# Differential attention: the first softmax map left undivided, the row norm's epsilon scaled to match, and the second map's separate scaling folded into the difference

## The chip, the cores and the metric

The kernel runs as one program on one core of a Trainium2 chip. Its time is the device time of one execution in microseconds (us). Three runs of the kernel before took 1530.87, 1522.81 and 1524.97 us; their median is 1524.97 us.

## The reference, cut to what matters

The network layer has three attention branches; the change is in branch A, differential attention, with 4 heads and 2 softmax maps each, over two groups of 512 tokens.

```python
logits = jnp.einsum('bqhmd,bkhmd->bhmqk', qb, k) * scale + bias
p = jax.nn.softmax(logits, axis=-1)
attn = p[:, :, 0] - lam * p[:, :, 1]
o = jnp.einsum('bhqk,bkhe->bqhe', attn, v)
o = rms_norm(o, subln_g) * (1.0 - lambda_init)   # mean square over 128 values, plus EPS = 1e-6
```

`lam` is one number for the layer. The softmax of a map is `exp(logits - max)` divided by the row's sum `z`; call the exponentials `e0`, `e1` and their sums `z0`, `z1`. Each row of `attn` is `e0/z0 - lam * e1/z1`. The row norm that follows divides by the root of the row's mean square, so a factor on a whole row falls out of it if EPS is multiplied by the square of that factor.

## The kernel before, in words

The work is written out by hand for five engines, each with its own list of instructions in `build_program`; they meet at semaphores. TensorE (PE) multiplies, ScalarE (ACT) takes exponentials and rounds operands to their high parts, VectorE (DVE) takes maxima, normalises and forms low parts, GpSimd (POOL) forms the low parts of weights (L450) and inverse roots (L436), SyncE (SP) issues the loads and stores. Every product is three products of high and low parts.

Branch A is a loop over 4 units (one head each, both its maps). Units 0 to 2 are a hardware loop, in which the counts that semaphores are compared with, and addresses that depend on the unit, come from registers; unit 3 is written out behind it. A unit goes through 8 tiles `t` of 128 query rows (4 in each token group), with two slots (`t % 2`) for scores and row statistics (`stat`). For one tile:

- PE: `score` (L611) makes the scores of both maps in PSUM.
- DVE: `find_max` adds the bias and takes each map's maximum (two instructions of L1383, into `s`), and L1388 negates the two maxima.
- ACT: `exp_probs` (L1017) takes both exponentials and, by an accumulator, the sums `z0`, `z1` (`stat` columns 4 and 5).
- DVE: `scales` takes both reciprocals (L1394, columns 6 and 7), waits for them (`steps.done`), and multiplies the second by `lam` (L1397, column 8).
- ACT: `scale_second` (L1038) multiplies the second map by column 8.
- DVE: `norm_probs` (L1411) waits for that (`scaled`) and writes `e0 * column 6 - scaled second map` in place of `e0`.
- PE: `turn_tile` turns the result into PSUM in four transposes (L618); ACT rounds it (`probs_hi`, L1029) and DVE takes the rest (`probs_lo`, L1355).
- PE: `mix` (L633) multiplies with the values, one token group at a time.

The order on the engines around it, in `attend_qkv`:

- DVE, step `t`: `scales(t-1)`, `find_max(t)`, `norm_probs(t-1)`, `probs_lo(t-2)`. At `t = 1` the low parts of the values follow (`v_lo`, L1355).
- ACT, step `t`: `probs_hi(t-2)`, `scale_second(t-1)`, `exp_probs(t)`; behind `exp_probs(3)` a weight block is rounded (`split_w`, L1002), and POOL's L450 follows from it.
- PE, step `t`: `turn_tile(t-2)`, `score(t+1)`, then shares of the gate's projection (L581), as many blocks as `GATE_SHARES_A = [1, 1, 2, 1, 1, 1, 1, 0]` says. After step 7 `finish` sets the next unit's projections between the last two `turn_tile`s.

`find_max(t)` may write its slot of `s` once tile `t-2` has been turned (`p_turned`). After each unit, PE sums the squares of the outputs (L720) and DVE copies 8 columns of sums to `a_ss` (L1486, an address that depends on the unit in the loop). After unit 3 `mean_square` (L1366) makes `a_ss / 128 + EPS` in one instruction on 32 columns, POOL raises it to the power -0.5 (L436), and DVE spreads the result over diagonals (L1634) that PE multiplies (L819).

Branches B and C (`both` is true) have two separate softmax maps. They use the same helpers, with `scale_second` (L1038) and a `norm_probs` of their own (L1408).

Of the kernel before, what the change touches and what calls it, by code (L numbers as in the profile page):

```python
# [28 lines left out]
ALU = mybir.AluOpType  # L29
# [3 lines left out]
P = 128  # L33
# [11 lines left out]
UNITS = 4  # L45
# [6 lines left out]
EPS = 1e-6  # L52
LAMBDA_INIT = 0.2
SCALE = HD ** -0.5
NEG = -3.0e38
LEAD = 8
# [22 lines left out]
def build_program(nc, w_qkvg_a, w_qg_b, w_qkvg_c, w_gates, w_branch, w_out, w_pg, w_pe,  # L79
# [3 lines left out]
    with ExitStack() as ctx:  # L83
# [25 lines left out]
        ident = sb("ident", [P, P])  # L109
        mask = sb("mask", [P, 3, 48])  # L110
        stat = sb("stat", [P, 2, 12])
        small = sb("small", [P, 128])
        ps = ctx.enter_context(nc.psum_tensor("ps", [P, 8, 512], F32))

        bias = tables[:, 0:2 * NBIAS].rearrange("p (e n) -> p e n", e=2)
# [3 lines left out]
        lambda_in = tables[:, 256:256 + 4 * HD]  # L119
        copy_of_x = [tables[:, c * TOK:(c + 1) * TOK] for c in range(2)]  # L120
        neg_half = small[:, 0:1]
        lam = small[:, 1:2]
        subg = small[:, 2:3]
        ones2 = small[:, 4:6]
        lam_sum = small[:, 6:8]
# [3 lines left out]
        a_ss = small[:, 32:64]  # L129
        a_rstd = small[:, 64:96]  # L130
        head_ss, head_rstd = small[:, 96:112], small[:, 112:128]

        const_in = sem("const_in")
        x_in = [sem(f"x_in{i}") for i in range(4)]
# [436 lines left out]
        def _(pe):  # L571
# [77 lines left out]
            def turn_tile(u, t, near, both):  # L649

                pe.wait_ge(normed, LEAD + 8 * u + t + 1)
                if both:

                    pe.wait_ge(pt0_ready, half_count(u, t, 0, both))
                    turn_probs(t, near, both, 0).then_inc(p0_turned, 1)
                    pe.wait_ge(scaled, LEAD + 8 * u + t + 1)
                    pe.wait_ge(pt_ready, half_count(u, t, 1, both))
                    turn_probs(t, near, both, 1).then_inc(p_turned, 1)
                else:
                    pe.wait_ge(pt_ready, LEAD + 8 * u + t - 1)  # L660
                    turn_probs(t, near, both, 0).then_inc(p_turned, 1)
# [326 lines left out]
        def _(act):  # L988
# [40 lines left out]
                    nc.scalar.copy(*turned_probs(pt_hi, j, near, both, e)) \  # L1029
                        .then_inc(pt0_hi_done if half0 else pt_hi_done, 1)  # L1030

            def scale_second(u, t, near, both):

                lo, hi = C_KEYS[t % QT] if near else (0, QT)
                act.wait_ge(scales_ready, LEAD + 8 * u + t + 1)
                p1 = s[:, t % 2, 1, 0:(hi - lo) * P]
                factor = stat[:, t % 2, 7:8] if both else stat[:, t % 2, 8:9]
                nc.scalar.mul(p1, p1, factor).then_inc(scaled, 1)  # L1038

            def gate_tanh(u, n_gate, bank):  # L1040
                act.wait_ge(block_done, LEAD + n_gate + 1)
# [26 lines left out]
            def attend_qkv(u, n, uses, near, both, gate_at, n_turned):  # L1068

                act.wait_ge(y_ready, LEAD + 2 * u)  # L1070
                save_plain(n + 2, 0, vg[:, :])
                for t in range(8):
                    if t >= 2:
                        probs_hi(u, t - 2, near, both)
                    if t >= 1:
                        scale_second(u, t - 1, near, both)
                    exp_probs(u, t, near, both)
                    if t == 0:
                        values_hi(u, n_turned, 0, both)
                    if t == 3:  # L1080
                        split_w(n + 4, 0, uses + 1)
                    if t == gate_at:
                        gate_tanh(u, n + 3, 2)
                    if t == gate_at + 1:
                        split_w(n + 5, 1, uses + 1)

            def finish(u, n, uses, near, both, gate_at):
                if gate_at == 8:
                    gate_tanh(u, n + 3, 2)
                    split_w(n + 5, 1, uses + 1)  # L1090
                scale_second(u, 7, near, both)
                probs_hi(u, 6, near, both)
                probs_hi(u, 7, near, both)

# [119 lines left out]
            def attend_b(i, last):  # L1214
                u = UNITS + i
                n, uses = N_B + 2 * i, N_B // 2 + 2 + i
                for t in range(8):
                    if t >= 2:
                        probs_hi(u, t - 2, False, True)
                    if t >= 1:  # L1220
                        scale_second(u, t - 1, False, True)
                    if t == 3 and not last:
                        act.wait_ge(rope_turned, LEAD + 2 + i)
                        save_plain(n, 2, rope_buf)
                    if t == 4 and not last:
                        square_heads(UNITS + 4 + i, 2, y_row(i + 1))
                    exp_probs(u, t, False, True)
                    if t == 1:
                        split_w(n + 1, 0, uses)
                    if t == 5 and not last:  # L1230
                        split_w(n + 2, 1, uses)
                scale_second(u, 7, False, True)
                probs_hi(u, 6, False, True)
                probs_hi(u, 7, False, True)
                gate_tanh(u, n + (0 if last else 1), 4)
                if last:
                    split_w(n + 2, 1, uses)
                if not last:
                    act.wait_ge(rope_turned, LEAD + 3 + i)
                    q_to_hi(u + 1, 6)  # L1240
# [112 lines left out]
        def _(dve):  # L1353
# [36 lines left out]
            def scales(u, t, both):  # L1390

                st = stat[:, t % 2, :]
                dve.wait_ge(exped, LEAD + 8 * u + t + 1)
                done = nc.vector.reciprocal(st[:, 6:8], st[:, 4:6])  # L1394
                if not both:
                    steps.done(dve, done)
                    done = nc.vector.tensor_tensor(st[:, 8:9], st[:, 7:8], lam, ALU.mult)  # L1397
                done.then_inc(scales_ready, 1)

            def norm_probs(u, t, near, both):  # L1400

                lo, hi = C_KEYS[t % QT] if near else (0, QT)
                width = (hi - lo) * P
                st = stat[:, t % 2, :]
                p0, p1 = s[:, t % 2, 0, 0:width], s[:, t % 2, 1, 0:width]
                if both:
                    dve.wait_ge(scales_ready, LEAD + 8 * u + t + 1)
                    nc.vector.tensor_scalar(p0, p0, st[:, 6:7], None, ALU.mult).then_inc(normed, 1)  # L1408
                else:
                    dve.wait_ge(scaled, LEAD + 8 * u + t + 1)  # L1410
                    stt(out=p0, in0=p0, scalar=st[:, 6:7], in1=p1, op0=ALU.mult, op1=ALU.subtract) \  # L1411
                        .then_inc(normed, 1)

            def probs_lo(u, j, near, both):
# [120 lines left out]
            nc.vector.tensor_reduce(lam_sum, prod, AX.X, ALU.add).then_inc(lam_summed, 1)  # L1535
            steps.done(dve, nc.vector.tensor_scalar(subg, subg, 1.0 - LAMBDA_INIT, None, ALU.mult))
            dve.wait_ge(lam_exped, LEAD + 1)
            steps.done(dve, nc.vector.tensor_tensor(lam, lam_exp[:, 0:1], lam_exp[:, 1:2], ALU.subtract))
            steps.done(dve, nc.vector.tensor_scalar(lam, lam, LAMBDA_INIT, None, ALU.add))

            def h_lo_part(t):
                dve.wait_ge(h_hi_done, LEAD + t + 1)
# [22 lines left out]

            first_qkv(0, 0)
            with dve.Fori(0, UNITS - 1) as i:
                steps.loop(i, 8 + 8)
                dve.wait_ge(bias_ready, LEAD + i + 1)
                attend_qkv(i, False, False, 8, i)  # L1570
                finish(i, False, False, 8)
                next_qkv(i, i, i, True)
                save_squares(i)
# [6 lines left out]
                take_y(last, last, g, True)  # L1580
            save_squares(last)
            dve.wait_ge(ss_saved, LEAD + UNITS)
            mean_square(a_ss, P, a_var)

            def rope_tables(n_in):
                dve.wait_ge(rope_in, 16 * n_in)
# [311 lines left out]
```

## Time and profile before

| what | value |
|---|---|
| median of the three runs | 1524.97 us |
| lowest and highest run | 1522.81 and 1530.87 us |
| span of the profiled execution | 1522.4 us |
| PE busy | 1411.3 us, 93% of the span, 6780 instructions |
| DVE busy | 602.4 us, 40%, 1062 instructions |
| ACT busy | 536.9 us, 35%, 977 instructions |
| POOL busy | 291.8 us, 19%, 173 instructions |
| mean granted TensorE clock | 0.973 of full speed |

The span runs from the first to the last instruction of one profiled execution; for that execution the page gives no other time. It lies 0.41 us below the lowest run and 2.57 us below the median. A busy share is an average over the whole program; what an edit in one stage is worth is read from that stage's own stretch.

In the answers of the trace, "idle before <-X" is how long the engine stood still ahead of an instruction and whose end released it. In the chain of waits, "issue" is time in which the engine waited for nothing that the profile shows.

### The profile page before, as it was taken

The page shows a single profiled execution, that of the slowest core. Times are in us where ns is not written, and L with a number is a line of the kernel's source. Part 1 is how long each engine was busy: PE and PEld are TensorE (multiplying, and loading weights), DVE is VectorE, ACT ScalarE, POOL GpSimd, SP SyncE. Part 2 cuts the span into 40 slices and gives each one's busy share as a digit, 9 for nine tenths or more (in the row PEclk, how much of TensorE's full clock was granted, in tenths as well). Part 3 has the DMA queues.
Part 4 walks back from the last instruction along what each step waited for, and adds up shares of the span by engine and source line. Part 5 has one row for each costly group of instructions (what it writes and reads, how often), then busy time and mean ns, then how long its engine had stood idle before and what let it go on. Part 6 is the DMA issues. An engine that isn't in the chain of part 4 may idle for free.

```text
span 1522.4 us, 18598 instructions
## 1 busy us (share of the span) xinstructions
PE 1411.3 (93%) x6780; PEld 1129.2 (74%) x6780; DVE 602.4 (40%) x1062; ACT 536.9 (35%) x977; POOL 291.8 (19%) x173
## 2 busy tenths in 40 slices
PE   5999999999999798987999898989898999899998
PEld 3767677677887576765788786878787888788887
DVE  5272635546300646456212125152525212544332
ACT  4262534432111536446211115252524212324432
POOL 1211202131222113020022131111211112213100
PEclk9999999999999999998999999999999999999999
DMA  5111101011111000000011110111000113322200
GB/s 185 57 36 36 49 21 49 28 45 46 42 42 55 28 14 28 14 14 8 21 43 61 55 56 23 46 34 34 34 28 29 42 42 138 111 82 70 69 35 35
DMA packets 25746, 71.77 MB, mean 47 GB/s; under 512 B 2872, under 2 KB 4792, under 8 KB 25568
## 3 DMA queue, kind: packets, MB, share of 16 engines
q1 hardware_dynamic: 25696, 71.09, 13.9%
q8 instruction: 33, 0.54, 0.2%
q14 instruction: 17, 0.14, 0.0%
HBM read 66.86 MB, written 4.23 MB: 47 GB/s over the span
## 4 chain that ended last, share of the span: by engine, by line
PE 84%; DVE 8%; ACT 3%; issue 3%; POOL 1%; DMA 0%; SPq 0%; DVEq 0%; ACTq 0%; POOLq 0%
PE ps L581 45%; PE ps L738 9%; PE ps L633 7%; PE ps L952 6%; PE ps L934 6%; PE ps L618 3%; PE ps L611 3%; ACT s L1017 2%; DVE s L1383 2%; PE ps L598 2%; PE ps L958 1%; DVE pt_lo L1355 1%; DVE stat L1388 1%; PE ps L764 1%; POOL small L436 1%
## 5 line engine op out<-in xcount | busy, mean ns | idle before, releaser
L450 POOL TENSOR_TENSOR w_lo<-stage,w_hi 128x1024 fp32r<-128x1024 f32 (+1 forms) x92 | 194.4, 2113 | 923.8 <-ACT w_hi L1002 922.6
L581 PE MATMUL ps<-h_hi,w_hi 128*128 128x512 f32 x1040 | 335.8, 404 | 4.2 <-ACT s L1017 1.9
L581 PE MATMUL ps<-h_lo,w_hi 128*128 128x512 f32 x1040 | 324.3, 393 | 0.0
L581 PE MATMUL ps<-h_hi,w_lo 128*128 128x512 f32 x1040 | 323.7, 393 | 0.0
L581 PEld LDWEIGHTS ps<-h_hi,w_hi 128*128 128x128 f32 x1040 | 188.6, 189 | 59.2 <-issue 19.7
L581 PEld LDWEIGHTS ps<-h_lo,w_hi 128*128 128x128 f32 x1040 | 196.5, 189 | 44.5
L581 PEld LDWEIGHTS ps<-h_hi,w_lo 128*128 128x128 f32 x1040 | 196.3, 189 | 43.3
L1002 ACT CAST w_hi<-stage 128x1024 fp32r<-128x1024 f32 (+1 forms) x92 | 86.0, 935 | 298.2 <-PE ps L581 213.1
L1029 ACT CAST pt_hi<-ps 128x512 fp32r<-128x512 f32 (+2 forms) x160 | 77.6, 525 | 167.6 <-PE ps L618 103.6
L1355 DVE TENSOR_TENSOR pt_lo<-ps,pt_hi 128x512 fp32r<-128x512 f32 (+2 forms) x160 | 91.3, 603 | 113.9 <-ACT pt_hi L1029 113.9
L618 PE MATMUL ps<-ident,s 128*128 128x128 f32 x544 | 85.6, 288 | 51.5 <-DVE pt_lo L1355 34.4
L618 PEld LDWEIGHTS ps<-ident,s 128*128 128x128 f32 x544 | 63.9, 146 | 80.7 <-DVE pt_lo L1355 32.1
L1383 DVE CUSTOM_DVE_ANT_0 s<-ps,tables 128x512 f32<-128x512 f32 (+2 forms) x128 | 70.5, 588 | 91.3 <-PE ps L611 64.0
L1017 ACT ACTIVATE s<-s,stat 128x512 f32<-128x512 f32 (+2 forms) x128 | 81.2, 636 | 55.0 <-DVE stat L1388 54.6
L1502 DVE SCALAR_TENSOR_TENSOR s<-s,ps 128x1024 f32<-128x1024 f32 x16 | 19.5, 1221 | 190.1 <-PE ps L738 190.1
L633 PE MATMUL ps<-pt_hi,v_hi 128*128 128x512 f32 (+2 forms) x192 | 71.0, 370 | 9.1 <-DVE pt_lo L1355 4.8
L738 PE MATMUL ps<-pt_hi,w_hi 128*128 128x512 f32 x192 | 61.7, 404 | 10.3 <-DVE m L1504 8.9
L633 PE MATMUL ps<-pt_lo,v_hi 128*128 128x512 f32 (+2 forms) x192 | 69.1, 360 | 0.0
L633 PE MATMUL ps<-pt_hi,v_lo 128*128 128x512 f32 (+2 forms) x192 | 68.6, 357 | 0.0
L1038 ACT ACTIVATE s<-s,stat 128x512 f32<-128x512 f32 (+2 forms) x96 | 65.0, 677 | 4.4 <-DVE stat L1394 4.4
L738 PE MATMUL ps<-pt_hi,w_lo 128*128 128x512 f32 x192 | 60.9, 399 | 0.0
L738 PE MATMUL ps<-pt_lo,w_hi 128*128 128x512 f32 x192 | 60.7, 398 | 0.0
(173 smaller groups left out, 1881.6 us busy)
## 6 DMA issues: line engine op xcount, KB each, us to landing
stage<-in_w_gates SPq DMA_DIRECT2D x24, 512.0 KB, 3.2
stage<-in_w_qkvg_a SPq DMA_DIRECT2D x19, 512.0 KB, 3.2
stage<-in_w_qkvg_c SPq DMA_DIRECT2D x16, 512.0 KB, 3.2
stage<-in_w_branch SPq DMA_DIRECT2D x24, 256.0 KB, 2.7
m<-in_x_tok SPq DMA_DIRECT2D x4, 1024.0 KB, 9.4
y<-in_x_tok SPq DMA_DIRECT2D x8, 512.0 KB, 3.4
stage<-in_w_pg SPq DMA_DIRECT2D x16, 256.0 KB, 2.7
out<-y SPq DMA_DIRECT2D x16, 256.0 KB, 2.0
```

Of the source, the lines that this page charges most:

```text
L450: nc.gpsimd.tensor_tensor(dst, stage[:, slot, 0:width], f32(hi), ALU.subtract).then_inc(w_ready, 1)
L581: done = mm(ps[:, bank + g, :], w[:, slot, k * P:(k + 1) * P], h[:, k, g * SEQ:(g + 1) * SEQ], start=first and part == 0, stop=last and pa ...
L618: done = nc.tensor.transpose(ps[:, e if both else t % 2, k * P:(k + 1) * P], s[:, t % 2, e, k * P:(k + 1) * P], ident[:, :])
L633: done = mm(ps[:, 2 + g, q0 * P:q1 * P], v[:, g * QT + k, e * HD:e * HD + P], p[:, e if both else g, k, q0 * P:q1 * P], start=n == 0, stop ...
L738: done = mm(ps[:, 2 + g, :], w[:, slot, c * P:(c + 1) * P], yy[:, c * TOK + g * SEQ:c * TOK + (g + 1) * SEQ], start=c == 0 and part == 0, ...
L934: done = mm(ps[:, 2 * c + nb, :], a[:, k * P:(k + 1) * P], w[:, k, nb * 512:(nb + 1) * 512], start=k == 0 and part == 0, stop=k == KC - 1 ...
L952: mm(ps[:, c, :], a[:, k * P:(k + 1) * P], w[:, k * 512:(k + 1) * 512], start=k == 0 and part == 0, stop=k == KC - 1 and part == 2)
L1002: nc.scalar.copy(dst, stage[:, slot, 0:width]).then_inc(w_hi_done, 1)
L1017: done = nc.scalar.activation(dst, src, ACT.Exp, bias=stat[:, t % 2, 2 + e:3 + e], accum_out=stat[:, t % 2, 4 + e:5 + e])
L1029: nc.scalar.copy(*turned_probs(pt_hi, j, near, both, e)) \
L1355: sub = lambda out, whole, hi: nc.vector.tensor_tensor(out, whole, f32(hi), ALU.subtract)
L1383: done = nc.vector.tensor_tensor_reduce(out=s[:, t % 2, e, 0:width], in0=ps[:, 4 + 2 * (t % 2) + e, 0:width], in1=bias[:, e, first:first + ...
```

## The change

For branch A (`both` false):

- `scales` takes the reciprocal of `z1` alone, then `z0 * (-lam) * (1/z1)` into column 8, then `z0 * z0` into a new column of `a_z`, at an address that depends on the unit and the tile. It waits for the first two results, one after the other; `scales_ready` is signalled by the third.
- `scale_second` is no longer issued on ACT for this branch.
- `norm_probs` writes `e1 * column 8 + e0` in place of `e0`, without the wait for `scaled`.
- Behind the branch, `mean_square` on `a_ss` becomes two instructions with a wait between them: `a_z * EPS`, then `a_ss / 128 + a_z`.
- `lam` is kept negated; `small` grows from 128 to 160 columns; the counts of `scaled` begin at branch B; the loop's step count per unit goes from 16 to 24.

For branches B and C the instructions are the same.

```diff
-        small = sb("small", [P, 128])
+        small = sb("small", [P, 160])
...
+        a_z = small[:, 128:160]
...
-                    pe.wait_ge(scaled, LEAD + 8 * u + t + 1)
+                    pe.wait_ge(scaled, LEAD + 8 * (u - UNITS) + t + 1)
...
-                factor = stat[:, t % 2, 7:8] if both else stat[:, t % 2, 8:9]
-                nc.scalar.mul(p1, p1, factor).then_inc(scaled, 1)
+                nc.scalar.mul(p1, p1, stat[:, t % 2, 7:8]).then_inc(scaled, 1)
...
-                    if t >= 1:
-                        scale_second(u, t - 1, near, both)
+                    if t >= 1 and both:
+                        scale_second(u, t - 1, near)
...
-                done = nc.vector.reciprocal(st[:, 6:8], st[:, 4:6])
-                if not both:
-                    steps.done(dve, done)
-                    done = nc.vector.tensor_tensor(st[:, 8:9], st[:, 7:8], lam, ALU.mult)
-                done.then_inc(scales_ready, 1)
+                if both:
+                    nc.vector.reciprocal(st[:, 6:8], st[:, 4:6]).then_inc(scales_ready, 1)
+                    return
+
+                steps.done(dve, nc.vector.reciprocal(st[:, 7:8], st[:, 5:6]))
+                steps.done(dve, stt(out=st[:, 8:9], in0=st[:, 4:5], scalar=neg_lam, in1=st[:, 7:8], op0=ALU.mult,
+                                    op1=ALU.mult))
+                nc.vector.tensor_tensor(a_z[:, bass.ds(8 * u + t, 1)], st[:, 4:5], st[:, 4:5], ALU.mult) \
+                    .then_inc(scales_ready, 1)
...
-                    dve.wait_ge(scaled, LEAD + 8 * u + t + 1)
-                    stt(out=p0, in0=p0, scalar=st[:, 6:7], in1=p1, op0=ALU.mult, op1=ALU.subtract) \
+                    stt(out=p0, in0=p1, scalar=st[:, 8:9], in1=p0, op0=ALU.mult, op1=ALU.add) \
...
-                steps.loop(i, 8 + 8)
+                steps.loop(i, 8 + 16)
...
-            mean_square(a_ss, P, a_var)
+            steps.done(dve, nc.vector.tensor_scalar(a_z, a_z, EPS, None, ALU.mult))
+            stt(out=a_ss, in0=a_ss, scalar=1.0 / P, in1=a_z, op0=ALU.mult, op1=ALU.add).then_inc(a_var, 1)
```

## Rows read from the trace of the kernel before

**Rows 1.** Engines by stretch: branch A's four units; busy us (instructions), then PEclk, DMA, GB/s.
```profile
core 0: us, PE busy (x) PEld busy (x) DVE busy (x) ACT busy (x) POOL busy (x), PEclk, DMA share, GB/s
68.61:139.97 71.36, 67.81 (x323) 52.44 (x322) 33.77 (x78) 32.24 (x60) 11.88 (x6) 0.95 0.11 38
139.97:209.38 69.41, 64.92 (x323) 50.12 (x322) 33.95 (x79) 31.18 (x59) 11.88 (x6) 1.00 0.11 38
209.38:280.63 71.25, 67.66 (x323) 52.16 (x322) 33.95 (x79) 31.24 (x59) 11.88 (x6) 0.95 0.10 33
280.63:334.95 54.32, 50.34 (x261) 38.25 (x261) 32.02 (x80) 28.19 (x56) 8.18 (x6) 1.00 0.13 42
```

**Rows 2.** Waits of PE, 68 to 340 us: us in total, times, longest us.
```profile
PE ps L618 <- DVE s L1411: 9.0, 8, 1.8
PE ps L618 <- DVE v_lo L1355: 6.6, 4, 1.7
```

**Rows 3.** Timeline of unit 1, tiles 4 to 6: start us, us, engine, line, operation.
```profile
163.46 0.72 ACT L1017 ACTIVATE s<-s,stat 128x512 f32<-128x512 f32 x1 [0.91 <-DVE stat L1388]
...
165.01 0.17 DVE L1394 RECIPROCAL stat<-stat 128x2 f32<-128x2 f32 x1 [0.33 <-ACT s L1017]
165.22 0.16 DVE L1397 TENSOR_TENSOR stat<-stat,small 128x1 f32<-128x1 f32 x1
165.41 0.72 ACT L1038 ACTIVATE s<-s,stat 128x512 f32<-128x512 f32 x1
165.49 0.69 DVE L1383 CUSTOM_DVE_ANT_0 s<-ps,tables 128x512 f32<-128x512 f32 x1
...
166.92 0.74 DVE L1411 SCALAR_TENSOR_TENSOR s<-s,stat 128x512 f32<-128x512 f32 x1
...
167.72 0.66 PE L618 MATMUL ps<-ident,s 128*128 128x128 f32 x4 [0.45 <-DVE s L1411]
```

**Rows 4.** Instructions of L1411: who it waited for, us in total and times.
```profile
  ACT s L1038: 1.4, 4
```

**Rows 5.** Instructions of L1486: those of its sequencer; ns min/median/max.
```profile
L1486 DVEq FUSED_REGOPS  x3: 57/57/57, 140.0 to 280.7; - x3
```

**Rows 6.** Timeline, where `find_max` waits for PE: unit 1 (tiles 2, 3), units 0, 2 (6).
```profile
149.07 0.69 DVE L1383 CUSTOM_DVE_ANT_0 s<-ps,tables 128x512 f32<-128x512 f32 x1 [0.70 <-PE ps L618]
...
153.35 0.69 DVE L1383 CUSTOM_DVE_ANT_0 s<-ps,tables 128x512 f32<-128x512 f32 x1 [0.81 <-PE ps L618]
...
96.09 0.69 DVE L1383 CUSTOM_DVE_ANT_0 s<-ps,tables 128x512 f32<-128x512 f32 x1 [0.46 <-PE ps L618]
...
236.75 0.69 DVE L1383 CUSTOM_DVE_ANT_0 s<-ps,tables 128x512 f32<-128x512 f32 x1 [0.43 <-PE ps L618]
```

**Rows 7.** Timeline of unit 0, tiles 3 and 4, beside POOL's weight split.
```profile
86.72 0.17 DVE L1394 RECIPROCAL stat<-stat 128x2 f32<-128x2 f32 x1 [0.34 <-ACT s L1017]
...
87.70 2.37 POOL L450 TENSOR_TENSOR w_lo<-stage,w_hi 128x1024 fp32r<-128x1024 f32 x1 [25.60 <-ACT w_hi L1002]
...
87.82 0.69 DVE L1383 CUSTOM_DVE_ANT_0 s<-ps,tables 128x512 f32<-128x512 f32 x1
...
88.55 1.55 DVE L1388 TENSOR_SCALAR stat<-stat 128x2 f32<-128x2 f32 x1
```

**Rows 8.** Chain that ended last: unit 3's start, and behind branch A: start us, us.
```profile
286.73 0.65 DVE s L1411
287.38 1.15 DVE v_lo L1355
...
334.69 0.19 DVE small L1366
...
334.95 5.43 POOL small L436
```

**Rows 9.** Timeline of unit 3, tile 7, beside POOL's weight split (begun at 314.15).
```profile
314.73 2.38 DVE L1411 SCALAR_TENSOR_TENSOR s<-s,stat 128x512 f32<-128x512 f32 x1 [0.34 <-ACT s L1038]
```

**Rows 10.** Chain that ended last, unit 0: the same six L581 matmuls at either clock.
```profile
92.48 2.86 PE ps L581 x6
...
96.81 1.59 PE ps L581 x6
```

More of the change, by code:

```diff
@@ L121, in build_program @@
         neg_half = small[:, 0:1]
-        lam = small[:, 1:2]
+        neg_lam = small[:, 1:2]
         subg = small[:, 2:3]
@@ L1030, in probs_hi, with scale_second @@
                         .then_inc(pt0_hi_done if half0 else pt_hi_done, 1)
-            def scale_second(u, t, near, both):
+            def scale_second(u, t, near):
                 lo, hi = C_KEYS[t % QT] if near else (0, QT)
@@ L1090, in finish @@
                     split_w(n + 5, 1, uses + 1)
-                scale_second(u, 7, near, both)
+                if both:
+                    scale_second(u, 7, near)
                 probs_hi(u, 6, near, both)
@@ L1220, in attend_b @@
                     if t >= 1:
-                        scale_second(u, t - 1, False, True)
+                        scale_second(u, t - 1, False)
                     if t == 3 and not last:
@@ L1231, in attend_b @@
                         split_w(n + 2, 1, uses)
-                scale_second(u, 7, False, True)
+                scale_second(u, 7, False)
                 probs_hi(u, 6, False, True)
@@ L1393, in scales @@
                 dve.wait_ge(exped, LEAD + 8 * u + t + 1)
-                done = nc.vector.reciprocal(st[:, 6:8], st[:, 4:6])
-                if not both:
-                    steps.done(dve, done)
-                    done = nc.vector.tensor_tensor(st[:, 8:9], st[:, 7:8], lam, ALU.mult)
-                done.then_inc(scales_ready, 1)
+                if both:
+                    nc.vector.reciprocal(st[:, 6:8], st[:, 4:6]).then_inc(scales_ready, 1)
[5 more added lines that the diff above has]
+                    .then_inc(scales_ready, 1)
             def norm_probs(u, t, near, both):
@@ L1537, in _ @@
             dve.wait_ge(lam_exped, LEAD + 1)
-            steps.done(dve, nc.vector.tensor_tensor(lam, lam_exp[:, 0:1], lam_exp[:, 1:2], ALU.subtract))
-            steps.done(dve, nc.vector.tensor_scalar(lam, lam, LAMBDA_INIT, None, ALU.add))
+            steps.done(dve, nc.vector.tensor_tensor(neg_lam, lam_exp[:, 1:2], lam_exp[:, 0:1], ALU.subtract))
+            steps.done(dve, nc.vector.tensor_scalar(neg_lam, neg_lam, -LAMBDA_INIT, None, ALU.add))
             def h_lo_part(t):
```

## The prediction, made before the changed kernel was run

> **What bounds the kernel now.** I read the page's engine shares first (PE is busy nearly throughout), then cut out the stretch that the change touches. The table of engines by stretch gives branch A's four units 266.3 us together, of which PE is busy 250.7 us [rows 1]. So 15.6 us of PE idleness is all that the change could ever win back there, apart from the clock: units 0 and 2 show a mean granted clock of 0.95 and last 71.36 and 71.25 us, unit 1 shows 1.00 and lasts 69.41 us.
>
> Next, who makes PE wait. It is always the transpose L618: 9.0 us in 8 waits for the difference L1411 and 6.6 us in 4 waits for the values' low part, which stands behind L1411 on DVE [rows 2]. Which engine makes L1411 late? The timeline of one tile shows a ring [rows 3]: the exponentials start at 163.46, both are over when the reciprocal starts at 165.01, L1397 follows at 165.22, `find_max` of the next tile at 165.49, then its negation, then the next tile's exponentials and L1411 at 166.92, and PE, idle for 0.45 us, turns at 167.72. What the reader should see is where L1038 lies: ACT runs it from 165.41 to 166.13, while DVE is inside `find_max`, and L1411 can't start before `find_max` is over anyway. ACT itself stands idle 0.91 us ahead of the exponentials, waiting for DVE. So the ring is DVE's small operations, `find_max` and the two exponentials; the scaling is beside it.
>
> **The change, part by part.**
>
> *L1038 removed, 32 times 0.72 us of ACT* [rows 3]. Worth nothing: its cover is `find_max`, and with the multiplication gone ACT waits longer for L1388. L1411 waited for it 1.4 us in 4 waits [rows 4], one per unit, at tile 7; there PE has two half projections to do before it needs the result, and L1411 is held by POOL's split in any case (2.38 us instead of 0.74, with POOL's instruction under way) [rows 9]. Bounds: 0 to 1.4 us gained; I take 0. The wait for `scaled` that goes with it was already met when L1411 came up. `norm_probs` stays one instruction of the same form and size: no change.
>
> *`scales` becomes longer, between the exponentials and `find_max`: this is in the ring.* Reciprocal, wait, L1397 was two dependent small operations; now there are three, two of them awaited. From the start of the reciprocal to the start of L1397 is 165.22 - 165.01 = 0.21 us, wait included [rows 3]. The new product with `-lam` costs that step once more: 0.21 us. The square has an address that depends on the unit: the one such instruction of this engine nearby has a register operation of 0.057 us ahead of it, in the 3 units of the loop only [rows 5]. The trace has no small instruction of this form, with a register operation between a wait and its start; lower end 0 (the register work hidden under the instruction before), upper end 0.11 us (it and as much again to start). I take 0.10. So a tile costs 0.31 us more in units 0 to 2 and 0.21 in unit 3.
>
> Not every tile pays. Which of `scales(0)` to `scales(5)` reach PE?
> - `scales(0)`: `find_max(1)`, L1411, the values' low part and PE's first turn follow without a gap (the end of that run is in the chain) [rows 8]. Paid in all 4 units.
> - `scales(1)` and `scales(2)`: `find_max` behind them stands idle 0.70 and 0.81 us for PE's transpose [rows 6]. The usual gap there is 165.49 - 165.38 = 0.11 [rows 3], so 0.59 and 0.70 us are free, more than 0.31. Hidden; if PE came sooner they would be paid.
> - `scales(3)`: the reciprocal starts at 86.72, POOL's weight split at 87.70, and L1388 then takes 1.55 us in place of 0.17 [rows 7]; all four units look so. L1388 ends when POOL does, and POOL's start hangs on the exponentials of tile 3, ahead of this `scales`. So 0.31 us goes into a hold of 1.38 us. Hidden.
> - `scales(4)` and `scales(5)`: in units 1 and 3 the ring is tight (rows 3 are such a tile): both paid. In units 0 and 2 PE runs half as fast here (six matmuls take 2.86 us, later 1.59 [rows 10]), and `find_max(6)` waits 0.46 and 0.43 us for it [rows 6], so 0.35 and 0.32 of the 0.62 us is free and 0.27 and 0.30 is paid.
> - `scales(6)` and `scales(7)`: PE has the unit's last projections to do. Hidden.
>
> Sum: units 0 and 2: 0.31 + 0.27 and 0.31 + 0.30; unit 1: 3 x 0.31 = 0.93; unit 3: 3 x 0.21 = 0.63. Together 2.8 us. With the register work at 0 it is 0.28 + 0.30 + 0.63 + 0.63 = 1.8 us, at 0.11 it is 2.9.
>
> *Behind branch A*, one instruction of 0.19 us ahead of the inverse roots becomes two with a wait, in the chain that ends last [rows 8]: 0.2 us more. The powers are of larger numbers now; the trace shows no dependence on the values, so their 5.43 us stays.
>
> *Semaphore counts, `neg_lam`, the larger tile*: set-up or bookkeeping of the same number of instructions elsewhere; 0.
>
> Total +3.0 us. On the profiled execution that is 1522.4 + 3.0 = 1525.4 us of span; this execution stands 2.57 us under the median of the runs, so the median should be 1524.97 + 3.0 = **1528.0 us**, 0.2% more. About 0.5% (7.6 us) is what a measurement of this kernel can tell from no change, so the forecast is no change.
>
> **The rivals.**
>
> *1. The clock falls in other units.* Units 0 and 2 lose 71.3 - 69.4 = 1.9 us to a clock that falls to 1.2 GHz after PE's idle time behind the first turns; unit 1, with nearly the same gaps, loses none [rows 1]. The new small waits lengthen gaps and shift them. If units 1 and 3 fall too, they pay 3.8 us but hide about half of their 1.6: some 1531.0 us. If units 0 and 2 stop falling, 3.8 us comes back and they pay 0.93 each in place of 0.6: 1524.9. For: the units alternate although their work is equal. Against: nothing in the change aims at it.
>
> *2. A new small operation is caught by POOL's weight split: slower.* Place: `scales(3)`. The square must have started before POOL does, 87.70 - 86.72 = 0.98 us after the reciprocal [rows 7]; I put it 0.52 us after. If it comes later than 0.98 us, it is held until POOL ends at 90.07, and `find_max(4)` with 1.35 us behind it, instead of L1388 alone; L1388 would end near 91.8 in place of 90.10, 1.7 us late in each of four units: 3.0 + 6.8 = 9.8 us, 1534.8. For: L1411, two inputs in SBUF, was held so [rows 9]. Against: 0.46 us of room, and `find_max` beside POOL is not held (0.69 us) [rows 7].
> The Trainium skill, "SBUF — State Buffer", section "Who interferes with whom", says that a VectorE instruction with two SBUF inputs contends with a GpSimd instruction that reads SBUF, and that the one that issues second fully blocks. Both new products are of that kind, and the row of the held L1411 agrees with it; by this rule they are safe only because they come first.
>
> *3. ACT was in the ring after all: faster.* If the scaling set L1411 at the tight tiles (3 in each unit), 12 x 0.72 = 8.6 us would come back, less the 3.0: 1519.4. Against: ACT's 0.91 us of idleness and DVE's order of work [rows 3].
>
> *4. Nothing hides: slower.* If the room behind PE and POOL is not there, 24 tiles pay 0.31 and 8 pay 0.21: 9.1 us, 1534.3. Against: rows 6 and 7.
>
> **How the numbers follow.** Forecast 0.66; clock falls added 0.10, falls lost 0.09; rival 2 0.05; rival 3 0.04; rival 4 0.04; 0.02 for what I don't see. Forecast and both clock cases end within 0.5% of 1524.97 (1517.3 to 1532.6). Rivals 2 and 4 end just beyond it: slower 0.09; faster 0.05; same 0.86. The range takes the forecast's bounds (1526.8 to 1528.1, less the 1.4 us at tile 7), both clock cases (1524.9 to 1531.0) and, since three runs of one program lay 8 us apart, some 2.5 us on either side: 1522.5 to 1533.5.
>
> **What would show it.** In the changed profile: three small DVE instructions between the exponentials and `find_max`, from the reciprocal's start to `find_max` some 0.8 us in the loop, where it was 0.48 (165.49 - 165.01); the second and third start 0.2 and 0.5 us after the first. ACT idle some 1.6 us ahead of the exponentials in place of 0.91. L1411's successor at tile 5 later against the unit's start by 0.6 to 0.9 us. Units of 71.9, 70.3, 71.9 and 54.9 us if the clock keeps its pattern. L1388 of tile 4 still ends with POOL. It is wrong if a unit becomes shorter at the same clock, if `find_max(4)` starts behind POOL, or if branches B and C change by more than the clock explains.

## The result, and the profile after

Six runs of the changed kernel took 1529.95 to 1535.46 us, median 1532.46; six of the kernel before on the same chip took 1522.81 to 1530.87, median 1524.95. The ratio is 1.0043, with a 95% interval from 1.0024 to 1.0061: slower by 0.2% to 0.6%. The prediction was 1528.0 us, with a range that ends at 1533.5.

The two profiled executions differ by 1528.2 - 1522.4 = 5.8 us of span. The table of engines by stretch shows branch A's four units of the changed kernel, to be held against [rows 1], with the same columns:

```profile
68.19:140.32 72.13, 67.81 (x323) 52.08 (x322) 35.40 (x86) 27.35 (x52) 11.87 (x6) 0.95 0.12 38
140.32:212.38 72.06, 66.45 (x323) 51.09 (x322) 35.64 (x87) 26.10 (x51) 11.86 (x6) 0.98 0.11 37
212.38:283.84 71.46, 67.85 (x323) 52.29 (x322) 35.63 (x87) 26.45 (x51) 11.87 (x6) 0.95 0.10 33
283.84:339.12 55.28, 51.76 (x263) 39.51 (x263) 34.03 (x89) 23.28 (x48) 8.16 (x5) 0.97 0.13 41
...
338.00:360.00 22.00, 19.76 (x110) 17.09 (x110) 13.55 (x40) 2.07 (x2) 10.62 (x3) 0.92 0.00 1
```

The units grew by 0.77, 2.65, 0.21 and 0.96 us, 4.6 together. Two things are mixed in that. PE's idle time in them went from 15.6 to 270.9 - 253.9 = 17.1 us, 1.5 more; PE's busy time for the same matmuls went from 250.7 to 253.9 us, 3.1 more, nearly all of it in units 1 and 3, whose granted clock is now 0.98 and 0.97 where it was 1.00. The last row is mostly the stretch behind branch A (the spread of the inverse roots, from 339.12 on), with a clock of 0.92. That stretch took 1.3 us longer than before. The start of the program gave 0.4 back; branches B and C differ by 0.3.

PE's waits in branch A (us in total, times, longest), against 9.0 in 8 and 6.6 in 4 before [rows 2]:

```profile
PE ps L619 <- DVE s L1415: 9.7, 8, 1.9
PE ps L619 <- DVE v_lo L1356: 7.3, 4, 2.1
```

The timeline (start us, us, engine, line, operation, idle time before) at three places: POOL's hold in unit 0, the ring in unit 1, the same tile in unit 3.

```profile
77.76 0.69 DVE L1384 CUSTOM_DVE_ANT_0 s<-ps,tables 128x512 f32<-128x512 f32 x1 [0.38 <-PE ps L619]
...
86.62 0.17 DVE L1399 RECIPROCAL stat<-stat 128x1 f32<-128x1 f32 x1 [0.34 <-ACT s L1018]
...
87.18 0.16 DVE L1402 TENSOR_TENSOR small<-stat 128x1 f32 x1
87.48 0.69 DVE L1384 CUSTOM_DVE_ANT_0 s<-ps,tables 128x512 f32<-128x512 f32 x1
87.60 2.37 POOL L451 TENSOR_TENSOR w_lo<-stage,w_hi 128x1024 fp32r<-128x1024 f32 x1 [25.93 <-ACT w_hi L1003]
...
88.82 1.18 DVE L1389 TENSOR_SCALAR stat<-stat 128x2 f32<-128x2 f32 x1
...
163.68 0.17 DVE L1399 RECIPROCAL stat<-stat 128x1 f32<-128x1 f32 x1 [0.33 <-ACT s L1018]
163.88 0.22 DVE L1400 SCALAR_TENSOR_TENSOR stat<-stat,small 128x1 f32<-128x1 f32 x1
164.24 0.16 DVE L1402 TENSOR_TENSOR small<-stat 128x1 f32 x1
164.53 0.69 DVE L1384 CUSTOM_DVE_ANT_0 s<-ps,tables 128x512 f32<-128x512 f32 x1
...
165.88 0.17 DVE L1389 TENSOR_SCALAR stat<-stat 128x2 f32<-128x2 f32 x1
165.96 0.75 DVE L1415 SCALAR_TENSOR_TENSOR s<-s,stat 128x512 f32<-128x512 f32 x1
166.09 0.72 ACT L1018 ACTIVATE s<-s,stat 128x512 f32<-128x512 f32 x1 [1.97 <-DVE stat L1389]
...
167.64 0.17 DVE L1399 RECIPROCAL stat<-stat 128x1 f32<-128x1 f32 x1 [0.33 <-ACT s L1018]
...
305.21 0.17 DVE L1399 RECIPROCAL stat<-stat 128x1 f32<-128x1 f32 x1 [0.33 <-ACT s L1018]
...
305.86 0.69 DVE L1384 CUSTOM_DVE_ANT_0 s<-ps,tables 128x512 f32<-128x512 f32 x1
```

In the ring [rows 3] the reciprocal now starts 164.53 - 163.68 = 0.85 us ahead of `find_max` (L1384), where it was 0.48, and ACT stands idle 1.97 us ahead of the exponentials, where it was 0.91 (the prediction said some 1.6). One ring, from reciprocal to reciprocal, lasts 167.64 - 163.68 = 3.96 us. In unit 3, which has no address from a register, the reciprocal starts 305.86 - 305.21 = 0.65 us ahead of `find_max`. The kernel before has, in unit 1 and then in unit 3:

```profile
168.60 0.17 DVE L1394 RECIPROCAL stat<-stat 128x2 f32<-128x2 f32 x1 [0.34 <-ACT s L1017]
...
305.27 0.17 DVE L1394 RECIPROCAL stat<-stat 128x2 f32<-128x2 f32 x1 [0.33 <-ACT s L1017]
...
305.66 0.69 DVE L1383 CUSTOM_DVE_ANT_0 s<-ps,tables 128x512 f32<-128x512 f32 x1
```

So its ring is 168.60 - 165.01 = 3.59 us [rows 3], and in unit 3 its reciprocal starts 305.66 - 305.27 = 0.39 us ahead. The view of the square's line (duration ns, lowest/median/highest) shows the register operation that only the loop has:

```profile
L1402 DVEq FUSED_REGOPS  x24: 57/57/71, 73.0 to 247.5; - x24
```

**How the runs are compared.** Runs of one program differ by 8 us and more, and a run's time follows its mean granted clock: 67 runs of the kernel before, in the three later comparisons, average 1530.9 us at a clock of 0.966, 1525.3 at 0.972 and 1522.8 at 0.975. So beside each ratio I give the difference from the kernel before at equal clock: one straight line for all runs (0.9 us for 0.001 of clock) and one level for each kernel, with 95% bounds. The runs lie 0.83 us (one standard deviation) about it. Each ratio, with its interval, is taken over all runs of its comparison, so it is not quite that of the two medians. For the changed kernel, 12 runs, that is **+4.6 +- 0.5 us**. Its plain mean is 6.5 us above that of before, 1532.8 against 1526.3, since its runs also have a lower clock: 0.9692 against 0.9712 on average, and none of 12 above 0.972, where 31 of 67 runs of before lie.

### The profile page after: what moved, and what is told of

It is laid out like the page before. It is cut to its first block, busy times and chain, and to the rows that moved or that the text cites. A ratio compares the mean times of both kernels' runs of the same rounds, so it can differ in the third digit from the quotient of the medians.

```text
span 1528.2 us, 18695 instructions
## 1 busy us (share of the span) xinstructions
PE 1413.8 (93%) x6780; PEld 1132.1 (74%) x6780; DVE 609.6 (40%) x1095; ACT 517.4 (34%) x945; POOL 291.5 (19%) x173
## 4 chain that ended last, share of the span: by engine, by line
PE 85%; DVE 7%; ACT 3%; issue 3%; POOL 1%; DMA 0%; SPq 0%; DVEq 0%; ACTq 0%; POOLq 0%
PE ps L582 46%; PE ps L739 9%; PE ps L634 7%; PE ps L953 6%; PE ps L935 6%; PE ps L619 4%; PE ps L612 4%; PE ps L599 2%; ACT s L1018 2%; PE ps L959 1%; DVE s L1384 1%; DVE pt_lo L1356 1%; PE ps L765 1%; DVE stat L1389 1%; PE ps L820 1%
## 5 line engine op out<-in xcount | busy, mean ns | idle before, releaser
L619 PE MATMUL ps<-ident,s 128*128 128x128 f32 x544 | 85.4, 289 | 54.9 <-DVE pt_lo L1356 36.9
L1018 ACT ACTIVATE s<-s,stat 128x512 f32<-128x512 f32 (+2 forms) x128 | 81.2, 636 | 77.6 <-DVE stat L1389 77.2
L1384 DVE CUSTOM_DVE_ANT_0 s<-ps,tables 128x512 f32<-128x512 f32 (+2 forms) x128 | 70.5, 588 | 89.1 <-PE ps L612 65.2
L1018 ACT ACTIVATE s<-ps,stat 128x512 f32<-128x512 f32 x64 | 43.7, 695 | 35.3 <-DVE stat L1377 35.3
```

Source lines behind the costliest of these rows:

```text
L619: done = nc.tensor.transpose(ps[:, e if both else t % 2, k * P:(k + 1) * P], s[:, t % 2, e, k * P:(k + 1) * P], ident[:, :])
L1018: done = nc.scalar.activation(dst, src, ACT.Exp, bias=stat[:, t % 2, 2 + e:3 + e], accum_out=stat[:, t % 2, 4 + e:5 + e])
L1384: done = nc.vector.tensor_tensor_reduce(out=s[:, t % 2, e, 0:width], in0=ps[:, 4 + 2 * (t % 2) + e, 0:width], in1=bias[:, e, first:first + ...
```

## The experiments

**The same kernel again.** No edit.

> The changed kernel itself, beside many runs of the kernel before on one chip, with the mean granted clock of every run. So far a line through all runs (one slope of time against granted clock for all kernels, a level of its own for each) puts the changed kernel 4.6 us above the kernel before at equal clock. Theory A: that holds, 4 to 5 us at equal clock, ratio 1.002 to 1.004, and the clocks of the two are spread alike, so the 7.5 us of the first comparison hold some 3 us of chance. Rival E (the change makes the clock fall more often): mean clock at least 0.002 lower than that of the kernel before, ratio 1.005 or more.

Six runs: 1533.35 us, ratio 1.0060 [1.0047, 1.0073]; at equal clock +4.5 +- 0.7. The level is the one that theory A named, but its other two signs failed, and both signs of rival E came: the ratio is above 1.005, and the mean clock is 0.9687 against 0.9727 for the kernel before in the same comparison, 0.004 lower. The kernel before itself averages 0.9697 in another comparison, so how much of that difference is the change's doing stays open. The profile has the same units to 0.1 us, the fall of the clock in units 1 and 3 among them. So that fall is not an accident of the first profile.

**Was ACT's scaling in the ring?** The kernel before with the scaling, and the wait for it, taken out of branch A (the diff is cut to its two main places).

> The kernel before, with the scaling of the second map by ScalarE left out (the second map stays an undivided exponential, not multiplied by lambda over its sum) and the wait for it. The ring on VectorE is as it was. Theory A: ScalarE's 32 x 0.72 us lie beside the maxima, so the time is that of the kernel before within 1.5 us (1523.5 to 1526.5). Rival D (the scaling was in the ring): up to 8.6 us less, 1516 us.

```diff
-                    if t >= 1:
+                    if t >= 1 and both:
                         scale_second(u, t - 1, near, both)
...
-                    dve.wait_ge(scaled, LEAD + 8 * u + t + 1)
                     stt(out=p0, in0=p0, scalar=st[:, 6:7], in1=p1, op0=ALU.mult, op1=ALU.subtract) \
```

Twelve runs: 1527.91 us, ratio 0.9997 [0.9979, 1.0015]; at equal clock 0.0 +- 0.5. PE's waits in branch A are those of [rows 2]:

```profile
PE ps L618 <- DVE s L1411: 9.0, 8, 1.9
PE ps L618 <- DVE v_lo L1356: 6.6, 4, 1.7
```

23 us of ACT's work are gone and nothing moved; neither did the 1.4 us at tile 7 [rows 4] come back. This shows that the scaling was worth nothing, so the loss belongs to what the change adds. This kernel's profile also has the low clock behind branch A, in work that it doesn't touch, from the same table by stretch:

```profile
334.00:360.00 26.00, 23.98 (x137) 20.98 (x137) 14.58 (x44) 2.07 (x2) 10.62 (x3) 0.93 0.00 1
```

The kernel before with one block moved (last experiment) has it there too: 26.7 us at 0.94 behind branch A, where the kernel before took 25.4 at 1.00; the changed kernel with two more squares has 25.4 at 1.00. So the 1.3 us there come and go without the change's operations, and I don't count them as its cost.

**Do all tiles pay, or some?** Two more awaited squares in `scales`, ahead of the one that the change adds (the loop's step count, which grows with them, is left out of the diff).

> The changed kernel with two more awaited squares of one column ahead of the maxima, on every tile of the first branch: about 0.4 us more in the ring. Theory A: units pay it at the tiles of factors 0, 4 and 5 and a little at 1 and 2, not at 3 (held by the weight split of GpSimd in any case), 1.4 us a unit, 5.6 us in all, 1538 us, and some more for the clock. Rival C (every tile pays): 32 x 0.4 = 12.8 us, 1545 us. Rival B (the ring costs little): under 2 us, 1533 to 1534 us.

```diff
+                for extra in range(2):
+                    steps.done(dve, nc.vector.tensor_tensor(st[:, 9 + extra:10 + extra], st[:, 4:5], st[:, 4:5], ALU.mult))
```

Eight runs: 1535.39 us, ratio 1.0043 [1.0027, 1.0060]; at equal clock +10.2 +- 0.6, 5.6 more than the changed kernel. The timeline of unit 1, and PE's waits:

```profile
162.79 0.16 DVE L1399 RECIPROCAL stat<-stat 128x1 f32<-128x1 f32 x1 [0.34 <-ACT s L1018]
...
163.24 0.35 DVE L1403 TENSOR_TENSOR stat<-stat 128x1 f32<-128x1 f32 x2
...
164.03 0.69 DVE L1384 CUSTOM_DVE_ANT_0 s<-ps,tables 128x512 f32<-128x512 f32 x1
```

```profile
PE ps L619 <- DVE s L1417: 13.8, 10, 1.8
PE ps L619 <- DVE v_lo L1356: 9.6, 4, 2.5
```

From the reciprocal to `find_max` it is 164.03 - 162.79 = 1.24 us here instead of 0.85, 0.39 more, about 0.2 for each awaited square. All 32 tiles would make that 12.5 us; the 5.6 at equal clock are 14 tiles' worth. Some tiles pay and others have room: theory A at equal clock, while the median stayed under its 1538 us, since these runs have a higher mean clock (0.9725) than those of the changed kernel. PE's waits grew from 17.0 to 23.4 us.

**The square out of the ring.** It goes behind the difference (L1413 here); the two awaited operations stay.

> The changed kernel with one move: the square z0*z0 (L1402) is issued behind the difference instead of ahead of the maxima. The ring from the exponentials to the next maxima then holds a reciprocal and one product, as before the change (0.48 us from the reciprocal's start to the maxima, perhaps 0.54 because the product takes 0.22 us in place of 0.16). Theory A (the longer ring is the direct cost, 0.37 us on the tiles that pay, and the idle time it adds makes the clock fall more often): most of the 7.5 us goes away, 1525 to 1528 us, and the falls of the clock in the first branch are about as few as before. Rival B (the longer ring costs little, the loss is at the end of the branch or in chance falls of the clock): it stays at 1530 to 1533 us.

```diff
-                nc.vector.tensor_tensor(a_z[:, bass.ds(8 * u + t, 1)], st[:, 4:5], st[:, 4:5], ALU.mult) \
-                    .then_inc(scales_ready, 1)
...
                     stt(out=p0, in0=p1, scalar=st[:, 8:9], in1=p0, op0=ALU.mult, op1=ALU.add) \
                         .then_inc(normed, 1)
+                    nc.vector.tensor_tensor(a_z[:, bass.ds(8 * u + t, 1)], st[:, 4:5], st[:, 4:5], ALU.mult) \
+                        .then_inc(scales_ready, 1)
```

Twelve runs: 1532.00 us, ratio 1.0029 [1.0015, 1.0042]; at equal clock +2.6 +- 0.5, so 2.0 us less than the changed kernel. Its timeline in unit 1:

```profile
163.59 0.16 DVE L1399 RECIPROCAL stat<-stat 128x1 f32<-128x1 f32 x1 [0.26 <-ACT s L1018]
163.78 0.22 DVE L1400 SCALAR_TENSOR_TENSOR stat<-stat,small 128x1 f32<-128x1 f32 x1
164.31 0.69 DVE L1384 CUSTOM_DVE_ANT_0 s<-ps,tables 128x512 f32<-128x512 f32 x1 [0.30 <-DVE stat L1400]
```

The square, its register operation and its start took 0.85 - 0.72 = 0.13 us of the ring, and no more: with it gone, `find_max` waits 0.30 us for the product, since the wait stands ahead of it in the list although `find_max` doesn't need the result. In unit 3, without registers, it waits 0.21:

```profile
307.48 0.69 DVE L1384 CUSTOM_DVE_ANT_0 s<-ps,tables 128x512 f32<-128x512 f32 x1 [0.21 <-DVE stat L1400]
```

Behind a square that isn't awaited, the changed kernel's `find_max` starts 0.13 us after the square's end in the loop (164.53 - 164.40) and 0.03 us in unit 3. So most of the price is the wait, some 0.2 us, and not the square's work. The Trainium skill, "VectorE: DVE Perf Modes", section "The DRAIN you can't avoid", says that a semaphore after each of a row of copies costs nothing extra, since the engine empties between them anyway. On operations this small the rows of the changed kernel differ: L1400 starts 163.88 - 163.68 = 0.20 us after the reciprocal that it awaits, and L1415 starts 165.96 - 165.88 = 0.08 us after L1389, for which it doesn't wait.

The median missed theory A's 1525 to 1528 us and lies in rival B's range; the 2.0 us at equal clock are real, but A's other sign failed outright. All four units of this profile have a lower clock (0.95, 0.95, 0.95 and 0.94), with PE's waits in branch A no longer than before the change (15.1 against 15.6 us):

```profile
PE ps L619 <- DVE v_lo L1356: 7.8, 4, 2.0
PE ps L619 <- DVE s L1413: 7.3, 4, 1.8
```

So shorter waits did not bring fewer falls of the clock.

**All three small operations out of ACT's ring.** `scales(t-1)` goes behind `find_max(t)` for branch A.

> The changed kernel with all three small operations of a tile behind the next tile's maxima instead of ahead of them, which is possible now that ScalarE no longer waits for the factor. The maxima then wait for the scores and the transposes alone, so the exponentials of the next tile need not wait for this tile's sums. Theory A: the tile's period is set by VectorE's own work, some 3.5 us in place of 3.95 (3.58 before the change), so it comes back to about the kernel before or a little under it: 1521 to 1527 us. Rival B: no more than 2 us under the changed kernel, 1530 to 1533 us.

```diff
-                    if t >= 1:
+                    if t >= 1 and both:
                         scales(u, t - 1, both)
                     find_max(u, t, near, both)
+                    if t >= 1 and not both:
+                        scales(u, t - 1, both)
```

Eight runs: 1537.34 us, ratio 1.0060 [1.0041, 1.0079]; at equal clock +8.4 +- 0.6. That is 3.8 more than the changed kernel, and outside the ranges of theory and rival alike. PE's waits:

```profile
PE ps L619 <- DVE s L1415: 13.0, 15, 1.9
PE ps L619 <- DVE v_lo L1356: 8.1, 4, 2.1
```

and the ring of unit 1 in the timeline:

```profile
164.43 0.69 DVE L1384 CUSTOM_DVE_ANT_0 s<-ps,tables 128x512 f32<-128x512 f32 x1 [0.29 <-issue]
...
167.28 0.66 PE L619 MATMUL ps<-ident,s 128*128 128x128 f32 x4 [0.54 <-DVE s L1415]
168.11 0.69 DVE L1384 CUSTOM_DVE_ANT_0 s<-ps,tables 128x512 f32<-128x512 f32 x1 [0.29 <-issue]
```

A ring of 168.11 - 164.43 = 3.68 us is shorter than the changed kernel's 3.96, and yet the time is longer: the small operations now stand straight ahead of the difference, and PE waits for it 15 times instead of 8, 21.1 us in all instead of 17.0. My reading, for which no run of its own was made: the idle time of `find_max`, which had hidden `scales(1)` and `scales(2)`, hides nothing that stands behind it.

**The reciprocal between the two maxima.** It goes between the two instructions of `find_max(t)`, the product behind them, the square behind the difference; no awaited operation is left ahead of `find_max`.

> The changed kernel with the small operations out of the way: the reciprocal between the two maxima of the next tile, the product behind them, the square behind the difference. The difference still comes behind the maxima, as in the kernel before; two of the three awaited steps now overlap with other work. Theory A: the ring from maxima through difference and transposes to the maxima after next is some 3.4 to 3.5 us (3.58 before, 3.95 changed), so 0 to 2 us below the kernel before at equal clock. Rival F (the product and its wait, now ahead of the difference, sit in a ring with PE's transposes as in the run with the factor behind the maxima, 8.3 us above at equal clock): 4 us or more above the kernel before.

```diff
+                    if e == 0 and t >= 1 and not both:
+                        before = stat[:, (t - 1) % 2, :]
+                        dve.wait_ge(exped, LEAD + 8 * u + t)
+                        nc.vector.reciprocal(before[:, 7:8], before[:, 5:6]).then_inc(dve_step, 1)
+                        steps.n += 1
...
-                steps.done(dve, nc.vector.reciprocal(st[:, 7:8], st[:, 5:6]))
+                if t == 7:
+                    dve.wait_ge(exped, LEAD + 8 * u + t + 1)
+                    steps.done(dve, nc.vector.reciprocal(st[:, 7:8], st[:, 5:6]))
```

Six runs: 1531.15 us, ratio 1.0046 [1.0031, 1.0061]; at equal clock +3.4 +- 0.7. Only 1.2 us less than the changed kernel, although the ring is much shorter (3.37 us; rows of the same ring stand with the last experiment). Theory A missed, and the result lies just under rival F's 4 us. Its four units all show falls of the clock (0.98, 0.95, 0.95 and 0.94).

**One block of the gate's projection one step earlier.** One of PE's two long waits in each unit stands at its first turns. Three kernels with one edit: the one before, the changed one, and the one with the reciprocal between the maxima.

> The kernel before with one block of the gate's projection moved from step 2 to step 1 of each unit, so that PE has 1.4 us of work while it waits 1.7 us for the first transposes of a unit. Theory A (PE's idle time there is what both costs time, since the second transposes and the maxima behind them then come 0.6 to 0.7 us earlier, and lets the clock fall): 2 to 3 us below the kernel before at equal clock, and fewer stretches at the low clock in units 0 and 2; 1520 to 1524 us. Rival G (the first transposes come later by what PE now does ahead of them): the same or up to 2 us slower.

> The changed kernel with the same move of one block. Theory A: 4 to 5 us above the kernel before with that move at equal clock, so about the time of the kernel before, 1525 to 1529 us; the longer ring is still paid, at the same tiles. Rival H (the loss came from PE's idle time behind the first transposes and the clock that falls there, not from the ring): within 1 us of the kernel before with that move.

> The version with the reciprocal between the maxima, whose ring takes 3.37 us (3.58 before) but which stood 3.3 us above the kernel before at equal clock with many stretches at the low clock in units 1 to 3, with the same move of one block. Theory A (its loss is the clock that falls in PE's gaps, so filling the first gap gives the shorter ring its worth): under the kernel before, 1519 to 1524 us. Rival I (it loses elsewhere): 1527 us or more.

```diff
-GATE_SHARES_A = [1, 1, 2, 1, 1, 1, 1, 0]
+GATE_SHARES_A = [1, 2, 1, 1, 1, 1, 1, 0]
```

| kernel with the earlier block, 12 runs each | median us | ratio to before | at equal clock, us |
|---|---|---|---|
| before | 1521.47 | 0.9973 [0.9960, 0.9986] | -3.0 +- 0.5 |
| changed | 1527.58 | 1.0013 [0.9999, 1.0027] | +2.1 +- 0.5 |
| reciprocal between the maxima | 1521.24 | 0.9974 [0.9959, 0.9989] | -2.2 +- 0.5 |

Engines by stretch, unit 1 of each, in this order:

```profile
136.62:205.33 68.71, 65.23 (x323) 50.04 (x322) 33.95 (x79) 31.10 (x59) 11.87 (x6) 1.00 0.12 39
```

```profile
138.62:208.84 70.22, 65.24 (x323) 50.04 (x322) 35.65 (x87) 26.02 (x51) 11.86 (x6) 1.00 0.11 38
```

```profile
139.45:207.99 68.54, 65.22 (x323) 50.05 (x322) 35.51 (x87) 26.48 (x51) 11.85 (x6) 1.00 0.12 39
```

The first two have a clock of 1.00 in all three units of the loop, so the price of the change stands alone: 70.22 - 68.71 = 1.51 us a unit, with PE's busy time equal. That is four tiles at the 0.37 us by which the changed kernel's ring is longer. The trace shows which: in unit 1, PE waits for DVE five times, and the waits go from 0.37, 0.37, 1.85, 0.44 and 0.45 us to 0.76, 0.75, 1.84, 0.82 and 0.81. The third is the tile that POOL's split holds; the others stand behind `scales(0)`, `(2)`, `(4)` and `(5)`. The totals in branch A agree; of the two kernels, before and changed:

```profile
PE ps L618 <- DVE s L1411: 11.5, 14, 1.8
...
PE ps L618 <- DVE v_lo L1355: 1.1, 3, 0.4
```

```profile
PE ps L619 <- DVE s L1415: 15.1, 14, 1.8
PE ps L619 <- DVE v_lo L1356: 2.6, 4, 0.8
```

17.7 - 12.6 = 5.1 us, and the levels at equal clock differ by 2.1 + 3.0 = 5.1. So here the loss is PE's waiting for the longer ring: theory A for all three kernels (5.1 us is just above its 4 to 5), and rivals G, H and I are out. Against the kernel before without the moved block, 15.6 - 12.6 = 3.0 us of waits are gone, the 3.0 us at equal clock. But the move doesn't keep the clock up everywhere: in unit 3 the kernel before now has 0.94, where it had 1.00, and the changed kernel 0.97. The third kernel does the changed arithmetic, and its unit 1 is 0.17 us shorter than the first's; its ring in the timeline:

```profile
163.79 0.69 DVE L1384 CUSTOM_DVE_ANT_0 s<-ps,tables 128x512 f32<-128x512 f32 x1 [0.22 <-issue]
...
164.41 0.16 DVE L1391 RECIPROCAL stat<-stat 128x1 f32<-128x1 f32 x1
164.48 0.67 DVE L1384 CUSTOM_DVE_ANT_0 s<-ps,tables 128x512 f32<-128x512 f32 x1
...
165.28 0.21 DVE L1407 SCALAR_TENSOR_TENSOR stat<-stat,small 128x1 f32<-128x1 f32 x1
165.52 0.75 DVE L1420 SCALAR_TENSOR_TENSOR s<-s,stat 128x512 f32<-128x512 f32 x1
...
167.16 0.69 DVE L1384 CUSTOM_DVE_ANT_0 s<-ps,tables 128x512 f32<-128x512 f32 x1 [0.22 <-issue]
```

The reciprocal lies inside `find_max`, its wait behind the second maximum; the ring is 167.16 - 163.79 = 3.37 us; the changed kernel has 3.96, the one before 3.59. The first and the third of these kernels beat the kernel before by 0.3% each, and so the changed one too; between the two I make no choice (0.2 us apart in the medians, and 0.8 the other way round at equal clock).

## Why the prediction was right or wrong, point by point

- *"L1038 removed ... Worth nothing"*: right, shown by the kernel without the scaling (0.0 +- 0.5 us). Rival 3 is out, and so is the 1.4 us at tile 7.
- *"`scales` becomes longer ... this is in the ring"*: right, and under-sized. A tile was put at 0.31 us more in the loop and 0.21 in unit 3; the rows show 0.85 - 0.48 = 0.37 and 0.65 - 0.39 = 0.26. The step of 0.21 us was copied from the reciprocal, which takes 0.17; the product with two tensors and a scalar takes 0.22. That is 0.05 of the 0.06. The second and third operation start 0.20 and 0.56 us after the first; 0.2 and 0.5 were foreseen.
- *"Not every tile pays"*: right, as the two more squares show (14 tiles' worth of 32). In unit 1 PE's waits grew at the three tiles that the list names: from 1.74, 0.44 and 0.45 us to 2.11, 0.83 and 0.83. "If PE came sooner they would be paid" came true as well: with the earlier block `scales(2)` is paid. The covers that the prediction named are in the rows: at tile 2 of unit 0 `find_max` still stands idle 0.38 us for PE's turn (0.70 before), and L1389 still ends with POOL, 1.18 us long where L1388 took 1.55. Rival 4 is out.
- *Rival 2* (the square caught by POOL) didn't happen: the square starts at 87.18 and ends at 87.34, POOL starts at 87.60.
- *"Behind branch A ... 0.2 us more"*: the stretch from the last squares to the powers grew by 0.22 us. Right.
- *"Units of 71.9, 70.3, 71.9 and 54.9 us if the clock keeps its pattern"*: this is the step that failed. They were 72.1, 72.1, 71.5 and 55.3, because the clock didn't keep it: it fell in units 1 and 3 as well, in both profiles of the changed kernel. That is rival 1, which got a chance of 0.10 and 1531.0 us. Its working holds: PE's busy time grew by 3.1 us (3.8 were put down for two falls), and its idle time by 1.5 only, since the slower PE hides part of the waits. In unit 3 this can be seen tile by tile: the first wait grew from 1.42 to 1.67 us, and the two of 0.36 us behind `scales(4)` and `(5)` are gone. L1411's successor at tile 5 of unit 1 came 2.6 us later against the unit's start, where 0.6 to 0.9 were foreseen: 1.1 from three longer waits, the rest from the clock. Against rival 1 the prediction wrote that nothing in the change aims at the clock. The change does lengthen waits after which the clock was seen to fall, but why it falls in more units stays open: with the square behind the difference the waits were no longer than before and it fell in all four, and in unit 2 of the changed kernel it fell at 214 us (0.50 from 214 to 216) without any wait of PE, which had been busy since 205 us and had taken the sums of squares (L721) from 210.5 to 212.3.
- *The sum*: 3.0 us were forecast; 4.6 +- 0.5 were measured at equal clock, 6.5 in the plain means. Working the prediction's own list of tiles again with 0.37 and 0.26 gives 0.76 + 1.11 + 0.79 + 0.78 + 0.2 = 3.6. A candidate for the further 1.0 us is the cover that a slow PE gave to units 0 and 2: with the earlier block, where no unit of the loop falls, four tiles of each pay, and the list has two for these units. The profile doesn't bear that out for unit 0, which grew by 0.77 us as the list has it; for the other runs it stays open, since longer waits and slower matmuls come together in them. The other 1.9 us are the lower mean clock of its runs.
- *The median as base*: the sum was put on a median of three runs, and three more gave the same. In the three later comparisons the median of before was 1529.41, 1524.77 and 1524.25 us, by the share of its runs at a lower clock; the range took in 2.5 us on either side for that, and the result lies inside, 1 us from its end. That it does is in part luck: without these 2.5 us it would have ended at 1531.0.
- *The chances*: "same" had 0.86, and the ratio 1.0043 lies within 0.5%, near its edge.

## What to carry to other kernels

In a ring that two engines pass to and fro, count the awaited small operations, not the work: on [128 x 1] each of those measured here (a reciprocal, a product, squares) cost about 0.2 us, and work taken off the engine that waits there anyway gave nothing back. Put such operations where the engine is inside something else (here between the two maxima), and ask who stands directly behind them. Give PE work for a long gap first: here one block of matmuls a step earlier won 2.5 to 5.6 us at equal clock, and only with it did the rearranged small operations beat the kernel before.

## What the runs showed of the hardware that was not expected

- An awaited operation on a 128 x 1 tile holds the engine's list even where the next instruction doesn't need it: `find_max` stands idle 0.30 us behind a product of 0.22 in the loop, and 0.21 in unit 3. Between the two maxima, with its wait met behind the second, the reciprocal costs the ring 164.48 - 164.41 = 0.07 us, the step from its start to the second maximum's.
- The clock's falls don't simply follow the length of the ring. 0.37 us more came with falls in units 1 and 3 (the changed kernel); 0.39 more again (two more squares) has none in unit 3, and 0.13 less (the square behind the difference) has them in all four units. With one block of matmuls moved by one step, units 1 and 2 have no fall in all three kernels, and unit 0 in two; in unit 3 the kernel before got one that it didn't have. No run here shows what decides it.
- The time of a run follows its mean granted clock at 0.9 us for each 0.001, so that medians of the kernel before in four comparisons lie up to 5 us apart. Differences under some 0.2% could be read only at equal clock.
